# A fourth buffer in the ring of level blocks of the gated recurrences

## What is computed

```python
def step(state, inp):
    qi, ki, vi, gi = inp
    bcum = jnp.cumsum(gi, axis=2)
    o_inter = jnp.einsum('bhtk,bhkv->bhtv', qi * jnp.exp(bcum), state)
    rel = bcum[:, :, :, None, :] - bcum[:, :, None, :, :]
    decay = jnp.exp(jnp.where(incl, rel, -jnp.inf))
    scores = jnp.einsum('bhtk,bhsk,bhtsk->bhts', qi, ki, decay)
    o_intra = jnp.einsum('bhts,bhsv->bhtv', scores, vi)
```

## Time and profile before

| what | value |
|---|---|
| median of 3 runs | 3206.66 us |
| range of the 3 runs | 3202.06 to 3206.76 us |
| time of the profiled execution | 3197.73 us |
| its span | 3196.4 us |
| PE busy | 2925.1 us, 92% of the span |
| DVE busy | 1608.7 us, 50% |
| ACT busy | 1033.5 us, 32% |
| POOL busy | 193.7 us, 6% |
| matmuls in the span | 18762 |

### The profile page before, as it was taken

One profiled execution on the slowest core, in us unless ns is written; L12 is line 12 of the kernel. 1 busy time (PEld: TensorE's weight loads), 2 busy tenths in 40 slices (PEclk: granted clock), 3 DMA queues, 4 the chain that ended last, 5 costly groups with the idle time before them and its releaser, 6 DMA issues.

```text
span 3196.4 us, 44835 instructions
## 1 busy us (share of the span) xinstructions
PE 2925.1 (92%) x18762; PEld 2401.2 (75%) x18762; DVE 1608.7 (50%) x3357; ACT 1033.5 (32%) x2010; POOL 193.7 (6%) x238
## 2 busy tenths in 40 slices
PE   7988999999999998898699999999899797899998
PEld 6766788888977566687558888888666687578886
DVE  4333544444445256676864424334825667654444
ACT  3223433233343145333243212212415444332222
POOL 0000000000000100100000000000211235100001
PEclk9999999999999999899799999999999798899999
DMA  7434312222222110222522122121111110223231
GB/s 235 152 108 159 105 54 60 60 60 60 72 87 105 53 34 1 83 80 81 171 81 92 40 79 66 53 69 56 55 52 34 30 41 1 93 92 106 92 99 60
DMA packets 227829, 248.74 MB, mean 78 GB/s; under 512 B 5569, under 2 KB 193069, under 8 KB 226093
## 3 DMA queue, kind: packets, MB, share of 16 engines
q1 hardware_dynamic: 227628, 245.89, 23.9%
HBM read 236.43 MB, written 9.44 MB: 77 GB/s over the span
## 4 chain that ended last, share of the span: by engine, by line
PE 56%; DVE 8%; ACT 3%; issue 2%; DMA 1%; POOL 0%; ACTq 0%; SPq 0%; DVEq 0%; POOLq 0%
PE PS L2183 53%; PE PS L2187 2%; PE PS L2394 2%; ACT AR L180 1%; DVE AR L3162 1%; DVE STAT L3098 1%; ACT L175 1%; DMA WR<-in_w_in 1%; DVE EX L3149 0%; DVE AR L2906 0%; ACT EX L180 0%; DMA WR<-in_w_mod 0%; DVE AR L2922 0%; ACT STAT L180 0%; DVE AR L3077 0%
## 5 line engine op out<-in xcount | busy, mean ns | idle before, releaser
L2183 PE MATMUL PS<-HI,WC 128*128 128x512 f32 (+2 forms) x1600 | 427.9, 353 | 0.7 <-DVE WC L3143 0.7
L2183 PE MATMUL PS<-AR 128*64 128x64 f32 (+7 forms) x3436 | 309.9, 272 | 62.9 <-ACT AR L180 24.9
L2183 PE MATMUL PS<-DW,DH 128*128 128x384 f32 (+1 forms) x1344 | 357.2, 348 | 0.9 <-DVE AR L2767 0.9
L180 ACT ACTIVATE AR<-PS 128x512 f32<-128x512 f32 (+4 forms) x389 | 165.9, 453 | 560.1 <-PE PS L2183 434.8
L2183 PEld LDWEIGHTS PS<-AR 128*64 128x64 f32 (+5 forms) x3436 | 261.1, 174 | 109.1 <-issue 33.8
L2183 PEld LDWEIGHTS PS<-HI,WC 128*128 128x128 f32 x1600 | 284.0, 189 | 42.4 <-DVE WC L3143 1.1
L2183 PE MATMUL PS<-LO,WC 128*128 128x512 f32 (+2 forms) x800 | 282.2, 353 | 0.0
L2183 PE MATMUL PS<-HT,WR 128*128 128x256 f32 (+1 forms) x928 | 261.7, 435 | 14.3 <-ACT EX L180 5.1
L2183 PE MATMUL PS<-WR,HT 128*128 128x128 f32 (+2 forms) x1296 | 251.2, 351 | 10.4 <-ACT AR L180 5.0
L2183 PEld LDWEIGHTS PS<-DW,DH 128*128 128x128 f32 x1344 | 242.1, 192 | 9.7 <-issue 7.1
L180 ACT ACTIVATE EX<-PS 128x256 f32<-128x256 f32 (+2 forms) x158 | 66.5, 430 | 533.8 <-PE PS L2183 533.7
(11 more groups left out here) (451 smaller groups left out, 4974.5 us busy)
## 6 DMA issues: line engine op xcount, KB each, us to landing
WR<-in_w_ffn_in SPq DMA_DIRECT2D x40, 1024.0 KB, 6.6
WR<-in_w_in_b SPq DMA_DIRECT2D x51, 512.0 KB, 6.1
WR<-in_w_mod SPq DMA_DIRECT2D x12, 2048.0 KB, 8.0
WR<-in_w_mod SPq DMA_DIRECT2D x24, 1024.0 KB, 5.3
WR<-in_w_ffn_out SPq DMA_DIRECT2D x22, 1024.0 KB, 5.0
WR<-in_w_in SPq DMA_DIRECT2D x40, 512.0 KB, 5.3
WR<-in_w_out SPq DMA_DIRECT2D x8, 2048.0 KB, 11.4
WR<-in_w_in SPq DMA_DIRECT2D x4, 2048.0 KB, 7.8
```

Source lines behind the costliest of these rows:

```text
L180: return self.o.activation(out, in_, func, **kw)
L2183: mm = lambda o, l, r, start, stop: e.o.matmul(o, l, r, start=start, stop=stop, skip_group_check=True)
```

## The change

The ring of level blocks gets a fourth block in both layers, from `early` in layer 0 and from `late` in layer 1. The new tile carries no point to wait for. In layer 0 `spare_at` is read after it and so moves up by 1792 columns. Nothing else is edited.

```diff
@@ -1732,6 +1732,7 @@
                 for ring in b_["DEC"]:
                     ring.until[0] = set_until[1]
             SQ = early.get(256)
+            hb[0]["X"].add((early.get if both else late)(7 * 256))
             spare_at = early.at
             prr, early_w = banks(6, 7), {}
             hpair, hturn, hout = Ring(pair(0), pair(2)), banks(4, 6) if both else banks(4, 6, 7), banks(5)
```

## The result

The changed kernel took 3183.47 us (median of 4 runs, 3180.9 to 3185.2) against 3204.36 us (median of 4 runs of the kernel before, 3199.73 to 3206.76): ratio 0.9936, interval 0.9919 to 0.9953, so 20.9 us or 0.64% faster. The kernel is faster, as forecast.

A forecast was written before the change was run, and what follows sets the result against it. PE, busy 92% of the span, was taken as the bound, standing still at two changes of heads in layer 0 through ACT's order. 7.1 + 7.1 = 14.2 us off 3206.7 gave 3192.5 us, range 3184 to 3203.

The forecast's parts named there:

- Where the waits are: First subtraction of `levels_begin`: DVE waits for the ring twice, 15.5 us together, both in layer 0, none in layer 1.
- The first change of heads: Layer 0, unit 8: PE's gap of 4.4 us and 2.7 us of half clock go, 7.1 us.
- The second change: Layer 0, unit 14: gap and half clock go, 7.1 us, with a margin of 0.2 us.
- What comes late next: Output end on DVE before the `ho` matmuls: over 2 us early at the first change, half a microsecond at the second.
- Whether it reaches the end: Behind the second change and to the end of the kernel: later stages the same, 14 us earlier.
- The clock: 16 projection matmuls behind each gap take 6.43 us at half clock, 3.72 at full: 2.7 us each.
- only the gaps go: Rival at both changes of heads: the clock falls all the same or elsewhere; gain 8.8 us, 3197.9 us, chance 0.12.
- slower: Rival: shifted timing tips 8 or more other PE gaps into costing clock, up to 2.7 us each; some 3214 us, 0.04.
- The forecast time and the range: Whole kernel: 3192.5 us, 0.44% off the median of 3206.7 us; range 3184 to 3203 us.
- The first case: Both changes of heads: both gaps and both half-clock stretches go; 3192.5 us, about 3186 to 3199, chance 0.68.
- the sum: Both changes of heads in layer 0 together: 7.1 + 7.1 = 14.2 us off.

The follow-up runs named there:

- layer 1 alone: Kernel before with the fourth block added to the ring in layer 1 only: 3200.38 us, ratio 1.0008.
- unit 8's wait put back alone: Changed kernel, but unit 8 waits for the multiplication of unit 5 again: 3191.39 us, ratio 0.9977 to the kernel before.
- three blocks and a later begin: Kernel before, second unit of layer 0's next head begun behind ACT's copy at both changes of heads: 3185.34 us, ratio 0.9957.
- the addresses alone: Kernel before with the fourth block's columns taken in both layers but not added to the ring: 3200.96 us, ratio 1.0002.
- the repeat: The changed kernel timed once more beside 23 runs of the kernel before: 3186.21 us, ratio 0.9955.
- the change a third time: The changed kernel timed a third time, 12 runs: 3186.93 us, ratio 0.9964 to the kernel before.
- layer 0 alone: Kernel before with the fourth block added to the ring in layer 0 only: 3186.34 us, ratio 0.9956.
- 4 copies: Changed kernel with 4 copies to unused columns on ACT behind the exponentials of units 8 and 14: 3193.81 us, ratio 0.9972.

## Why the prediction was right, and where it was wrong

*Where the waits are.* Right: two, in layer 0, at units 8 and 14, and none in layer 1. The kernel with layer 1 alone has no gain.

*The first change of heads,* 7.1 us. Right: 7.2 in the trace, and with unit 8's wait put back alone the stretch is 7.4 us longer. The step from DVE's wait over ACT's order to PE's bank is the one that the kernel with three blocks and a later begin shows.

*The second change,* 7.1 us with a margin of 0.2. Right: 7.2, with a margin of 0.1.

*What comes late next.* Right: nothing. The output end was done at 1355.1 in the changed kernel, 4.6 us before the output matmuls; the bound that I worked out gave over 2. At the second change it is closer: the output end is done on DVE at 1440.94, 0.3 us before the matmuls of 1441.21, where I had worked out half a microsecond.

*Whether it reaches the end.* Right, by the marks of SyncE's queue, through the stretch in which DVE is the busy engine. The 2 us more up to the end of layer 0 I did not have, and they aren't the change's: from the output matmuls of the second change to the first load of `x_spill` it is 146.9, 147.2 and 148.6 us in the three profiles of the changed kernel, 148.9 and 149.2 in the two of the kernel before, and 146.4 in the kernels with layer 1 and with the addresses alone.

*The clock,* 2.7 us each. Right in size: 6.38 to 6.71 us for the 16 matmuls behind all eleven gaps of 4.40 or 4.41 us, in seven traces. The rival "only the gaps go" fell with it, and "slower" too. But the mechanism on which "slower" rests, a gap that costs clock in one execution and not in another, is real; the last section shows one.

*The forecast time and the range* are where it was wrong. The step that failed is "The first case's own spread is 2.7 us of clock either way and the median's own uncertainty of some 3 us". The gain of 14.2 us stands, by the 14.4 us of the traces; the term that was mis-sized is the base. The forecast took 14.2 us from 3206.7 us, the median of three runs of the kernel before, and took that for the kernel's time within 3 us. Over the four sets of 17 to 26 runs that I have now the median is 3199.7 to 3200.6 us, so the base was 6 us too high; and single executions spread much more than the three had shown, from 3191.1 to 3210.0 us for the kernel before. The changed kernel's median of the first four runs, 3183.5, is the lowest of its three (3186.2 and 3186.9 later). By these longer sets the two together make the 9 us. Within the first comparison alone, where the base was 3204.4, the 9 us split otherwise: 2.3 us of base, and 6.7 us by which the measured difference exceeds the sum. By the terms alone, 3200.6 - 14.2 = 3186.4 us, which is what the later sets have. The profiled execution, 9 us below the median shown, had said that the three runs might lie high; I noted the difference and didn't use it.

What the size of the gain is: 14.4 and 12.8 us by the difference of medians in the longer sets, 14.2 by the sum. Why the first timing showed 20.9 isn't settled. Its interval, a gain of 15 to 26 us, meets that of the repeat, 11 to 18, so chance is enough for it. No experiment found a second effect. The two profiled executions of that timing differ by 14.9 us of span, and 14.4 us is what they differ by in the stretch that the change acts on. That the rest was chance is still argued and not shown.

## What to carry to other kernels

When an engine waits for a buffer, follow its queue to the engine behind it: the wait cost PE nothing by itself, and 7 us by what stood behind it on ACT. Such a wait can be taken away by a buffer or by moving the step behind the copy that matters, and the second was as good here. And a gain of 0.4% needs more than three runs of the base: put the sum on the base that the most executions give, the profiled one among them, and make the range wide enough for it. To see what a change of a few us is worth, compare the stretch that it acts on in the traces: there kernels of one kind agreed within 0.2 us (but for the one gap below), where whole executions moved by 20.

## What the runs showed that I had not expected

Executions of one kernel differ by far more than its first three runs tell. The profiled execution of the third set of the changed kernel has a span of 3203.4 us, where that of the first had 3181.5; the 12 runs of that set go from 3177.9 to 3204.7 us. The load that the changed kernel issues at 1348.70 us, ahead of everything that the change touches, comes at 1360.73 in the slower one: 12 of the 22 us are lost before. The granted clock over the whole span is 0.952 there against 0.960. That holds for the rest too: of the 21 executions of the changed kernel, the five slowest (3188.5 to 3204.7 us) are the five with a clock of 0.956 or less, and the other 16 (3177.9 to 3188.4 us) have 0.958 or more.

One gap shows how such differences can arise. Some 30 us behind the first change of heads PE waits for ACT for 3.00 us, in every trace, and then does 32 matmuls (the earlier trace rows has it at 1390.44). In the first profile of the changed kernel and in its third:

```profile
1385.33 5.44 PE L2184 MATMUL PS<-WR,HT 128*128 128x128 f32 x32 [2.99 <-ACT AR L180]
```

```profile
1397.36 3.81 PE L2184 MATMUL PS<-WR,HT 128*128 128x128 f32 x32 [3.00 <-ACT AR L180]
```

It is the same program, with the same gap, and the gap costs 1.6 us of clock in one execution and nothing in the other. Over all 17 traces the 32 matmuls take 5.44 us in 13, 5.30 in one, and 3.81 in three: the change a third time, layer 0 alone, and 4 copies. These are the three that stood apart in the table of the stretch: with 1.6 us added they have 91.5, 91.8 and 99.2, where the change has 91.7 and the sum for 4 copies gives 99.2.

So whether a gap of this length costs clock is not decided by its length alone. The gaps made with copies say the same: 3.14 us cost 1.6 us of clock, 3.20 cost 2.9, and 4.95 cost 2.1. Only the eleven gaps of 4.4 us cost much the same each time, 2.7 to 3.0 us. The Trainium skill (TensorE: Matmul & The Clock Gate, "What's actually happening") says that the activity window of the clock gate is free-running; by that, what a gap costs would depend on when it falls, and a gap that costs 1.6 us in one execution and nothing in another agrees with it. That such gaps make up the whole spread between executions isn't shown.
